# One ring of ten places for the expert weights of a mixture-of-experts layer, filled in the order of use

## The chip, the core and the metric

The kernel runs on one NeuronCore of a Trainium2 chip. The metric is the device time of one execution in microseconds (us); a kernel is judged by the median of its runs. Everything is float32.

## What is computed

One layer of an encoder trunk on 256 tokens of width 1024: a token mixer (differential attention and stick-breaking attention, behind an adaLN-conditioned RMSNorm), then a mixture of experts, then a final RMSNorm. Only the mixture of experts matters here. Each token goes to 4 of 32 experts:

```python
logits = (t @ router_w + router_b); top_val, top_idx = top_k(logits, 4); gates = softmax(top_val)
for each expert e, over the tokens xe that chose it:
    g, u = split(xe @ w_gu[e] + b_gu[e])            # w_gu[e]: 1024 x 2048
    g = minimum(g, 7); u = clip(u, -7, 7)
    y = ((u + 1) * (g * sigmoid(1.702 * g))) @ w_down[e] + b_down[e]   # w_down[e]: 1024 x 1024
    out[tokens] += gate * y
```

The weights of one expert are 12 MB (8 MB of `w_gu`, 4 MB of `w_down`), of all 32 experts 384 MB (402.7 million bytes). All of them are read, whatever the tokens choose.

## The kernel before, in words

The kernel is written engine by engine, with semaphores by hand. The token mixer comes first and ends some 400 us into the span; the expert part follows on the same buffers.

**Pieces and places.** SP (SyncE) issues all weight loads, each a piece of 2 MB: four pieces of `w_gu` and two of `w_down` per expert (`load_gu`, L378; `load_down`, L384). `gu_ring` is 16 MB: two halves of four places each. `down_ring` is 4 MB: two places. Expert e has its `w_gu` pieces in half e mod 2, and its `w_down` pieces in the two places of `down_ring`, as all experts have. So ten pieces fit at a time.

**TensorE, one expert** (`expert`, L1615). It takes the `w_gu` pieces in order (L1624; a wait on `slot_in` before each, L1634), eight k-tiles of 128 rows, with `give` of the former expert between (L1612) and `take` of the next one's tokens behind (L1582). After each second k-tile it raises `gu_used` so that a place becomes free. Then come the eight k-tiles of `w_down` (L1661; a wait on `down_in` before each half, L1659), with `down_used` behind each half. A matmul of 64 token places by 512 columns in float32 is two instructions of TensorE in the trace.

**Further passes.** An expert's main pass has 64 token places (`CAP`). If more tokens chose it, `further` (L1667) runs once for each 32 more, behind a branch on a count from memory (L346): matmuls with the same `w_gu` pieces again (L1691) and `w_down` (L1704), then the main pass's `w_down` part. The code of `further` stands in each copy of `expert`; where it isn't needed, TensorE jumps over it. With these inputs one expert, number 25 counted from 0, needs one such pass.

**TensorE's loop** (L1732) holds two experts, one for each half of `gu_ring`, and runs 16 times. VectorE and ScalarE have loops of one expert.

**The order of SP's loads.** SP issues in program order, and each issue waits until TensorE is done with the piece that stood there. For the first 16 experts the order is: `w_gu` of expert e+1, then `w_down` of expert e (L481 to L485). Around expert 16 a stretch written out moves each `w_down` piece one place ahead per expert (L486 to L493). From expert 21 on the order is `w_gu` of e, `w_down` of e (L497 to L500), where the two `w_down` pieces wait for `down_used` of the expert before. The first issue for an expert also waits for `f_gu_done`, so that no further pass still reads the place (L463 to L466).

Of the kernel before, what the change touches and what calls it, by code (L numbers as in the profile page):

```python
# [31 lines left out]
P = 128  # L32
D = 1024
T = 256
KT = D // P
# [4 lines left out]
NE, TOPK = 32, 4  # L40
# [19 lines left out]
FURTHER_BLOCKS = (T - CAP) // FCAP  # L60
PAIRS = NE // 2
TOGETHER = NE // 2

# [20 lines left out]
def build(nc, x, c, w_ada, b_ada, norm1_g, w_in, lam_q1, lam_k1, lam_q2, lam_k2, subln_g, w_pa, w_pb, w_o,  # L84
          norm2_g, router_w, router_b, w_gu, b_gu, w_down, b_down, final_g, out):
    ctx = ExitStack()
    with ctx:
# [103 lines left out]
        vt_pairs = xn[0:12, 1, 0:2 * P]  # L191
        fgb = xn[:, 0, :]
        bgu_rows = gu_ring[:, 11, 0:512]
# [140 lines left out]

        USES = [7] * 4 + [8] * 4 + [0] * 8

# [40 lines left out]
        def _(sp):  # L377
            def load_gu(expert, half, j):  # L378
                first = 8 * half + 2 * j
                sp.dma_start(gu_ring[:, first:first + 2, :].rearrange("p r n -> p (r n)"),  # L380
                             w_gu[0, bass.ds(expert, 1), j * 2 * P:(j + 1) * 2 * P, :]
                             .rearrange("a (p r) n -> p (a r n)", r=2)).then_inc(slot_in[first], 16)

            def load_down(expert, a):  # L384
                sp.dma_start(down_ring[:, 2 * a:2 * a + 2, :].rearrange("p s n -> p (s n)"),
                             w_down[0, bass.ds(expert, 1), a * 4 * P:(a + 1) * 4 * P, :]
                             .rearrange("a (p r) n -> p (a r n)", r=4)).then_inc(down_in[a], 16)

# [21 lines left out]
            for n, (w, g) in enumerate(GROUPS):  # L410
                if n < 2:
                    continue
                if n == len(GROUPS) - 1:
                    sp.wait_ge(sbpv_done, SBH)
                    for half in range(2):
                        sp.dma_start(y_sb[64 * half:64 * half + NE, :], b_down[0, :, half * 512:(half + 1) * 512]
                                     ).then_inc(bdown_in, 16)
                    for a in range(2):
                        load_down(0, a)
                    load_gu(1, 1, 0)  # L420
                if n >= 4:
# [19 lines left out]
            for j in range(4):  # L441
                if j == 2:
                    sp.wait_ge(merged_ready, 4)
                    for pair in (2, 3):
                        load_gu(1, 1, pair)
# [4 lines left out]
                load_gu(0, 0, j)  # L450
            sp.wait_ge(x1_ready, 4)
            sp.wait_ge(g2b_done, 1)
            load_gu(1, 1, 1)

            def load_item_gu(item, half):

                for j in range(4):
                    load_gu_pair(item, half, j)

            def load_gu_pair(item, half, j):  # L460

                if j == 0:
                    passes_made = sp.value_load(passes[0:1, 2, bass.ds(item - 1, 1)], min_val=1, max_val=T * TOPK // FCAP + 1)  # L463
                sp.wait_ge(gu_used, item * 8 + (2 * j - 14))
                if j == 0:
                    sp.wait_ge(f_gu_done, passes_made)  # L466
                load_gu(item, half, j)

            def load_down_half(item, a):

                sp.wait_ge(down_used, item * 2 + (a - 1))
                load_down(item, a)

            def load_item_down(item):
                for a in range(2):
                    load_down_half(item, a)

            sp.wait_ge(passes_ready, 1)
            load_item_gu(2, 0)
            load_item_down(1)  # L480
            with sp.Fori(1, TOGETHER // 2) as n:  # L481
                load_item_gu(n * 2 + 1, 1)
                load_item_down(n * 2)
                load_item_gu(n * 2 + 2, 0)
                load_item_down(n * 2 + 1)  # L485
            for step in range(4):  # L486
                item = TOGETHER + step
                for j in range(4):
                    if j == 3 - step:
                        load_down_half(item, 0)  # L490
                    load_gu_pair(item + 1, (item + 1) % 2, j)
                    if j == min(3, 4 - step - (step > 0)):
                        load_down_half(item, 1)  # L493
            load_item_down(TOGETHER + 4)
            load_item_gu(TOGETHER + 5, 1)
            load_item_down(TOGETHER + 5)
            with sp.Fori(TOGETHER // 2 + 3, PAIRS) as n:  # L497
                for half in range(2):
                    load_item_gu(n * 2 + half, half)
                    load_item_down(n * 2 + half)  # L500
            sp.wait_ge(taken_done, NE + 1)
            sp.dma_start(fgb, final_g.partition_broadcast(P)).then_inc(fg_in, 16)
# [711 lines left out]
        def _(pe):  # L1214
# [399 lines left out]

            def expert(item, half, fills):  # L1615

                count = further_count(pe, item)
                pe.wait_ge(xTe_ready, item + 1)

                def gate_up(kt, parts):  # L1620

                    for f in parts:
                        a = f % 2
                        last = M(bank[f // 2][64 * a:64 * a + 64, :], xT[:, kt % 4, kt // 4, :],  # L1624
                                 gu_ring[:, 8 * half + kt, f * 512:(f + 1) * 512],
                                 start=kt == 0, stop=kt == KT - 1, skip_group_check=True)
                    if f == 3:
                        last.then_inc(gu_used, 1)
                    elif kt == KT - 1:
                        last.then_inc(g_done, 1)  # L1630

                for kt in range(KT):
                    if kt % 2 == 0:
                        pe.wait_ge(slot_in[8 * half + kt], fills * 16 + 16 * USES[8 * half + kt])  # L1634
# [16 lines left out]
                way_back(item)  # L1651
                further_passes(pe, item, count, lambda b, k: further(item, half, fills, k))
                for kt in range(KT):
                    if kt == KT // 2:
                        take_transposed(item + 1)
                    if kt % (KT // 2) == 0:
                        pe.wait_ge(act_ready, item * 2 + (1 + 2 * kt // KT))
                    if kt % 4 == 0:
                        pe.wait_ge(down_in[kt // 4], item * 16 + 16)  # L1659
                    for a in range(2):  # L1660
                        last = M(bank[7][64 * a:64 * a + 64, :], act_sb[:, kt % 4, kt // 4, :],  # L1661
                                 down_ring[:, kt // 2, (kt % 2) * D + a * 512:(kt % 2) * D + (a + 1) * 512],
                                 start=kt == 0, stop=kt == KT - 1, skip_group_check=True)
                    if kt % 4 == 3:
                        last.then_inc(down_used, 1)

            def further(expert, half, fills, k):  # L1667

# [20 lines left out]
                for kt in range(KT):  # L1689
                    for f in range(4):  # L1690
                        last = M(bank[0][FCAP * f:FCAP * (f + 1), :], f_xT[:, kt % 2, kt // 2, :],  # L1691
                                 gu_ring[:, 8 * half + kt, f * 512:(f + 1) * 512],
                                 start=kt == 0, stop=kt == KT - 1, skip_group_check=True)
                last.then_inc(f_gu_done, 1)
# [4 lines left out]
                for kt in range(KT):  # L1699
                    if kt % 4 == 0:  # L1700
                        pe.wait_ge(down_in[kt // 4], expert * 16 + 16)
                    for a in range(2):
                        row = 64 * a + FCAP * (kt % 2)
                        last = M(bank[7][row:row + FCAP, :], f_act_sb[:, kt % 4, kt // 4, :],  # L1704
                                 down_ring[:, kt // 2, (kt % 2) * D + a * 512:(kt % 2) * D + (a + 1) * 512],
                                 start=kt < 2, stop=kt >= KT - 2, skip_group_check=True)
                last.then_inc(f_down_done, 1)
# [23 lines left out]
            pe.wait_ge(passes_ready, 1)  # L1731
            with pe.Fori(0, PAIRS) as n:  # L1732
                for half in range(2):
                    expert(n * 2 + half, half, n + 1)
            give(NE - 1)
# [19 lines left out]
```

## Time and profile before

| | |
|---|---|
| median of 3 runs | 1336.17 us (1335.73 to 1341.78) |
| span of the profiled execution | 1337.1 us |
| TensorE matmul (PE) busy | 1281.4 us, 96% |
| VectorE (DVE) busy | 518.3 us, 39% |
| ScalarE (ACT) busy | 187.3 us, 14% |
| read from HBM | 476.1 MB, 357 GB/s over the span |

The time of the profiled execution is not given apart from its span; the span, from the first to the last instruction, stands 0.9 us above the median of the runs. The expert part begins at 407 us (first matmul with `w_gu` of expert 0) and ends with the last instruction, so it is 930 us of the span. PE is the matmul part of TensorE, PEld its weight load; SPq is SP's sequencer issuing DMAs. A busy PE may still be a PE that is paced by its loads: whether it stands still shows in the idle time before an instruction, and in the chain of waits.

### The profile page before, as it was taken

To read this page: it belongs to the slowest core of one execution; us is meant where nothing else is said; L and a number is where in the kernel's file an instruction comes from. 1 tells how busy PE (TensorE), PEld (TensorE's weight loads), DVE (VectorE), ACT (ScalarE), POOL (GpSimd) and SP (SyncE) were. 2 spreads that over 40 slices of the span, in tenths; PEclk is the share of its full clock that TensorE was granted. 3 is DMA by queue.
4 is the path that set the end of the run, shared out by engine and by line. 5 is a ranking of instruction groups with operands and counts; after the bars stand their busy time and mean duration, and the time that the engine had idled before them with its cause. 6 is when DMAs were issued, how large, how long until landed. Compare 5 with 4: busy or idle time off the path is not lost.

```text
span 1337.1 us, 16781 instructions
## 1 busy us (share of the span) xinstructions
PE 1281.4 (96%) x5991; PEld 592.9 (44%) x5992; DVE 518.3 (39%) x1160; ACT 187.3 (14%) x381; POOL 15.6 (1%) x48
## 2 busy tenths in 40 slices
PE   6999999999999999999999999999999999899997
PEld 4866866778753333333333333333333333233332
DVE  3132665332234443444334334433434334334344
ACT  2101322332021001100001000000100011001002
POOL 0000000110000000000000000000000000000000
PEclk9999999999999999999999999999999999999999
DMA  9858675316678999999999999999999999799994
GB/s 355 318 189 291 223 245 186 126 64 230 231 287 318 425 428 428 428 428 429 428 428 429 429 428 429 428 428 428 414 429 428 428 429 428 315 430 427 428 430 210
DMA packets 59183, 477.55 MB, mean 357 GB/s; under 512 B 4991, under 2 KB 5076, under 8 KB 32532
## 3 DMA queue, kind: packets, MB, share of 16 engines
q1 hardware_dynamic: 58852, 476.11, 86.7%
q10 hardware_dynamic: 304, 1.06, 0.2%
q8 instruction: 19, 0.31, 0.1%
q14 instruction: 8, 0.07, 0.0%
HBM read 476.10 MB, written 1.05 MB: 357 GB/s over the span
## 4 chain that ended last, share of the span: by engine, by line
PE 74%; DMA 20%; DVE 3%; issue 1%; ACT 1%; SPq 0%; ACTq 0%; DVEq 0%
PE bank L1624 23%; DMA down_ring<-in_w_down 17%; PE bank L1661 15%; PE bank L1306 11%; PE bank L1452 4%; PE bank L1299 4%; PE bank L1612 3%; PE bank L1590 3%; DMA gu_ring<-in_w_gu 3%; PE bank L1354 2%; PE bank L1515 2%; PE bank L1582 1%; PE bank L1413 1%; DMA xres<-in_x 1%; DVE scratch L1137 1%
## 5 line engine op out<-in xcount | busy, mean ns | idle before, releaser
L1624 PE MATMUL bank<-gu_ring,scratch 128*64 128x512 f32 x2048 | 461.2, 597 | 1.7 <-DVE scratch L1067 1.6
L1624 PEld LDWEIGHTS bank<-gu_ring,scratch 128*64 128x64 f32 x2048 | 143.7, 137 | 286.3 <-issue 285.3
L1661 PE MATMUL bank<-down_ring,scratch 128*64 128x512 f32 x1024 | 235.5, 602 | 23.2 <-DMA down_ring<-in_w_down 18.0
L1306 PE MATMUL bank<-gu_ring 128*128 128x256 f32 x640 | 143.8, 381 | 0.0
L1661 PEld LDWEIGHTS bank<-down_ring,scratch 128*64 128x64 f32 x1024 | 71.0, 137 | 145.5 <-issue 133.5
L1306 PEld LDWEIGHTS bank<-gu_ring 128*128 128x128 f32 x640 | 119.8, 190 | 18.6 <-issue 1.3
L718 ACT ACTIVATE scratch<-bank 128x512 f32<-128x512 f32 x32 | 19.1, 597 | 686.5 <-PE bank L1624 686.5
L1125 DVE TENSOR_TENSOR scratch<-bank,bgu 128x512 f32<-128x512 f32 x32 | 22.1, 692 | 219.7 <-PE bank L1590 219.7
L1093 DVE TENSOR_TENSOR xres<-xres,bank 128x512 f32<-128x512 f32 x132 | 81.9, 682 | 60.1 <-PE bank L1612 60.1
L1590 PEld LDWEIGHTS bank<-ident,scratch 128*128 128x128 f32 x392 | 41.1, 140 | 79.5 <-issue 26.0
L1582 PE MATMUL bank<-xn,onehot 128*64 128x512 f32 x264 | 69.6, 605 | 0.0
L1066 DVE TENSOR_TENSOR scratch<-bank,a 128x512 f32<-128x512 f32 x33 | 22.8, 692 | 114.5 <-PE bank L1590 114.5
L1612 PE MATMUL bank<-scratch,back 64*128 64x512 f32 x264 | 65.6, 615 | 0.8 <-DVE scratch L1143 0.8
L1590 PE MATMUL bank<-ident,scratch 128*128 128x128 f32 x392 | 64.2, 286 | 0.7 <-ACT scratch L734 0.7
L1452 PE MATMUL bank<-gu_ring 128*128 128x256 f32 x256 | 56.4, 380 | 0.0
L1299 PE MATMUL bank<-gu_ring 128*128 128x512 f32 x128 | 55.8, 592 | 0.0
L1143 DVE TENSOR_TENSOR scratch<-bank,scratch 128x512 f32<-128x512 f32 x32 | 22.1, 692 | 79.8 <-PE bank L1661 79.8
L1452 PEld LDWEIGHTS bank<-gu_ring 128*128 128x128 f32 x256 | 48.3, 190 | 7.2 <-ACT gu_ring L671 0.5
L1113 DVE TENSOR_SCALAR gated<-iota,r,gates 128x64 f32<-128x64 f32 x128 | 40.3, 315 | 8.5 <-DVE gated L1113 6.1
L1612 PEld LDWEIGHTS bank<-scratch,back 64*128 64x128 f32 x264 | 22.7, 186 | 43.2 <-issue 41.5
L1135 DVE TENSOR_TENSOR scratch<-bank,bgu 128x256 f32<-128x256 f32 x64 | 26.9, 421 | 24.7 <-PE bank L1590 24.7
L1299 PEld LDWEIGHTS bank<-gu_ring 128*128 128x128 f32 x128 | 24.0, 190 | 28.2 <-issue 28.2
(265 smaller groups left out, 824.8 us busy)
## 6 DMA issues: line engine op xcount, KB each, us to landing
gu_ring<-in_w_gu SPq DMA_DIRECT2D x128, 2048.0 KB, 23.9
down_ring<-in_w_down SPq DMA_DIRECT2D x64, 2048.0 KB, 17.2
gu_ring<-in_w_in SPq DMA_DIRECT2D x32, 1024.0 KB, 7.8
gu_ring<-in_w_ada SPq DMA_DIRECT2D x16, 1024.0 KB, 7.0
down_ring<-in_w_ada SPq DMA_DIRECT2D x8, 512.0 KB, 10.6
gu_ring<-in_w_ada SPq DMA_DIRECT2D x8, 512.0 KB, 11.6
gu_ring<-in_w_pa SPq DMA_DIRECT2D x4, 1024.0 KB, 6.4
gu_ring<-in_w_pb SPq DMA_DIRECT2D x4, 1024.0 KB, 6.4
```

What stands on the lines that cost most here:

```text
L1093: V.tensor_tensor(xres[:, tt, cols], xres[:, tt, cols], bank[4 + n][:, :], ALU.add).then_inc(given_added, 1)
L1113: last = V.tensor_scalar(gated[:, tt, a, :], iota[:], r1[:, tt, bass.ds(item, 1)], gates[:, tt, bass.ds(item, 1)], ALU.is_equal, ALU.mult)
L1135: own.then(V.tensor_tensor(u, blocks(3)[:, :, a, :], u_bias, ALU.add))
L1299: last = M(dst[:, :], hT[:, kt, h * P:(h + 1) * P], group_chunk(group, kt // 4)[:, kt % 4, :], start=kt == 0, stop=kt == KT - 1)
L1306: last = M(dst[:, b * T:(b + 1) * T], group_chunk(group, kt // 4)[:, kt % 4, cols], hT[:, kt, :], start=kt == 0, stop=kt == KT - 1)
L1354: last = M(dst[:, b * T:(b + 1) * T], group_chunk(POS["in", g], a)[:, kt % 4, (2 * h + b) * P:(2 * h + b + 1) * P], hT[:, kt, :], start=kt ...
L1452: last = M(dst[:, b * T:(b + 1) * T], group_chunk(group, kt // 4)[:, kt % 4, (2 * h + b) * P:(2 * h + b + 1) * P], src[:, kt, :], start=kt ...
L1582: last = M(bank[4][64 * a:64 * a + 64, :], onehot[:, tt, :], xn[:, tt, a * 512:(a + 1) * 512], start=tt == 0, stop=tt == TT - 1, skip_grou ...
L1590: last = nc.tensor.transpose(bank[b][:, j * P:(j + 1) * P], src[:, j * P:(j + 1) * P], ident[:])
L1612: M(bank[4 + n][:, :], back[rows_, tt * P:(tt + 1) * P], y_sb[rows_, :], start=True, stop=True).then_inc(given_done, 1)
L1624: last = M(bank[f // 2][64 * a:64 * a + 64, :], xT[:, kt % 4, kt // 4, :], gu_ring[:, 8 * half + kt, f * 512:(f + 1) * 512], start=kt == 0 ...
L1661: last = M(bank[7][64 * a:64 * a + 64, :], act_sb[:, kt % 4, kt // 4, :], down_ring[:, kt // 2, (kt % 2) * D + a * 512:(kt % 2) * D + (a + ...
```

## The change

The two halves of `gu_ring` and the two places of `down_ring` become one ring of ten places. Piece n of the whole run is piece n mod 6 of expert n div 6 (four of `w_gu`, then two of `w_down`), and it goes to place `PLACES[n mod 10]`. Since 30 pieces are the least common multiple of 6 and 10, the places repeat every five experts: TensorE's loop holds five copies of `expert` and runs 6 times, and two more copies stand behind it. SP's loads are one function, `refill`: it waits until piece n-10 has been used, and issues piece n; there is no other order. The first ten pieces go to the same places at the same points of the program as before. The waits on landings (`wait_piece`) count the uses of each place. `final_g` is loaded to a free place of the ring, behind `down_used` of expert 30, instead of to `xn`. ScalarE's, VectorE's and GpSimd's programs are the same but for where `final_g` is read.

```diff
-PAIRS = NE // 2
-TOGETHER = NE // 2
+PIECES, GU_PIECES = 6, 4
+PLACES = (0, 1, 2, 3, 8, 9, 4, 5, 6, 7)
+CYCLE = 5
...
-        fgb = xn[:, 0, :]
+        fgb = gu_ring[:, 4, 0:D]
...
+        def area(place):
+
+            return gu_ring[:, 2 * place:2 * place + 2, :] if place < 8 else down_ring[:, 2 * place - 16:2 * place - 14, :]
...
+        def wait_piece(eng, piece, rounds):
+
+            place = place_of(piece)
+            eng.wait_ge(place_in(place), rounds * 48 + 16 * (USES[place] + piece // len(PLACES) + 1))
...
+            def refill(piece, rounds):
+
+                before_it = piece - len(PLACES)
+                former, i = before_it // PIECES + rounds * CYCLE, before_it % PIECES
+                if i == 0:
+                    passes_made = sp.value_load(passes[0:1, 2, bass.ds(former + 1, 1)], min_val=1, max_val=T * TOPK // FCAP + 1)
+                if i < GU_PIECES:
+                    sp.wait_ge(gu_used, former * 8 + (2 * i + 2))
+                else:
+                    sp.wait_ge(down_used, former * 2 + (i - GU_PIECES + 1))
+                if i == 0:
                     sp.wait_ge(f_gu_done, passes_made)
-                load_gu(item, half, j)
...
+                load_piece(rounds * CYCLE + piece // PIECES, piece % PIECES, place_of(piece))
 
             sp.wait_ge(passes_ready, 1)
...
+            for piece in range(len(PLACES), CYCLE * PIECES):
+                refill(piece, 0)
+            with sp.Fori(1, NE // CYCLE) as n:
+                for piece in range(CYCLE * PIECES):
+                    refill(piece, n)
+            for piece in range(NE % CYCLE * PIECES):
+                refill(piece, NE // CYCLE)
+            sp.wait_ge(down_used, 2 * NE - 2)
             sp.dma_start(fgb, final_g.partition_broadcast(P)).then_inc(fg_in, 16)
...
-            with pe.Fori(0, PAIRS) as n:
-                for half in range(2):
-                    expert(n * 2 + half, half, n + 1)
+            with pe.Fori(0, NE // CYCLE) as n:
+                for e in range(CYCLE):
+                    expert(e, n)
+            for e in range(NE % CYCLE):
+                expert(e, NE // CYCLE)
             give(NE - 1)
```

**SP, the loads that take the first places TensorE frees** (expert 0's four `w_gu` places, then its two `w_down` places; in brackets the semaphores waited for). Before:

```order
L463 TENSOR_LOAD passes [waits passes_ready]
L463 ISA x2
L380 DMA gu_ring<-in_w_gu 128x4096 [waits f_gu_done,gu_used]
L380 DMA gu_ring<-in_w_gu 128x4096 [waits gu_used] x3
L385 DMA down_ring<-in_w_down 128x4096 [waits down_used] x2
```

Now:

```order
L477 TENSOR_LOAD passes [waits passes_ready]
L477 ISA x2
L401 DMA gu_ring<-in_w_down 128x4096 [waits f_gu_done,gu_used]
L401 DMA gu_ring<-in_w_down 128x4096 [waits gu_used]
L401 DMA gu_ring<-in_w_gu 128x4096 [waits gu_used] x2
L401 DMA down_ring<-in_w_gu 128x4096 [waits down_used] x2
```

The events waited for are the same six in the same order. What is loaded at them differs: the `w_down` pieces of expert 1 come ahead of the `w_gu` pieces of expert 2.

**TensorE, the end of the second copy of `expert`** (its `w_down` part, with the transposes of the next expert's tokens between). Before, the loop ends there:

```order
L1661 MATMUL bank<-down_ring,scratch 64x512 x8
L1590 MATMUL bank<-ident,scratch 128x128 x4
L1661 MATMUL bank<-down_ring,scratch 64x512 x8
L1732 REGISTER_ALU
L1732 COMPARE_AND_BRANCH
L1612 MATMUL bank<-scratch,back 128x512 x4
```

Now the third of five copies follows, and the `w_down` pieces lie in `gu_ring`:

```order
L1668 MATMUL bank<-gu_ring,scratch 64x512 x8
L1583 MATMUL bank<-ident,scratch 128x128 x4
L1668 MATMUL bank<-gu_ring,scratch 64x512 x8
L360 ISA
L360 TENSOR_LOAD passes
L360 ISA x2
L351 REGISTER_ALU
L1632 MATMUL bank<-gu_ring,scratch 64x512 x8
L1605 MATMUL bank<-scratch,back 128x512 x4
```

The matmuls of one expert are as many and as large as before; the branch back comes after five experts instead of two.

## Rows read from the trace of the kernel before

**Rows 1.** The page, section 2: GB/s in 40 equal slices of the span.
```profile
GB/s 355 318 189 291 223 245 186 126 64 230 231 287 318 425 428 428 428 428 429 428 428 429 429 428 429 428 428 428 414 429 428 428 429 428 315 430 427 428 430 210
```

**Rows 2.** Busy time by stretch: length, each engine's us (x instructions), PEclk, DMA share, GB/s.
```profile
430.00:930.00 500.00, 480.34 (x2218) 165.99 (x2216) 195.54 (x459) 44.92 (x85) 0.00 (x0) 1.00 1.01 428
930.00:950.00 20.00, 19.81 (x97) 6.74 (x93) 7.06 (x16) 2.65 (x5) 0.00 (x0) 1.00 0.97 401
950.00:1130.00 180.00, 178.77 (x829) 60.14 (x826) 72.29 (x170) 17.64 (x33) 0.00 (x0) 1.00 1.01 429
1150.00:1160.00 10.00, 8.24 (x42) 3.02 (x40) 4.62 (x8) 0.00 (x0) 0.00 (x0) 1.00 0.28 80
1160.00:1316.00 156.00, 155.06 (x721) 52.17 (x717) 62.75 (x148) 14.99 (x28) 0.00 (x0) 1.00 1.00 427
```

**Rows 3.** The same view: one early expert, one later expert, the first 400 us.
```profile
428.64:456.02 27.38, 27.19 (x127) 9.21 (x127) 11.15 (x27) 2.65 (x7) 0.00 (x0) 1.00 1.01 424
...
538.14:565.51 27.37, 27.18 (x126) 9.20 (x127) 11.09 (x27) 2.64 (x7) 0.00 (x0) 1.00 1.01 429
...
0.00:400.00 400.00, 384.92 (x1791) 285.00 (x1792) 145.22 (x275) 93.90 (x201) 15.61 (x48) 1.00 0.63 228
```

**Rows 4.** The chain that ended last: start us, us, what.
```profile
620.26 3.65 PE bank L1661 x16
...
628.26 24.61 DMA down_ring<-in_w_down
...
912.82 3.65 PE bank L1661 x16
...
1088.15 35.68 DMA gu_ring<-in_w_gu
1123.87 2.80 PE bank L1624 x12
```

**Rows 5.** L380's issue at 1088.1 and L385's last issue: duration ns, start; time to landing.
```profile
L380 SPq DMA_DIRECT2D gu_ring<-in_w_gu x1: 333/333/333, 1088.1 to 1088.1; - x1
...
DMA to landing us min/median/max: 35.7/35.7/35.7
...
L385 SPq DMA_DIRECT2D down_ring<-in_w_down x1: 332/332/332, 1298.8 to 1298.8; - x1
...
DMA to landing us min/median/max: 19.2/19.2/19.2
```

**Rows 6.** PE's timeline: start us, us, line, operation, count, idle before and its releaser.
```profile
1117.54 9.13 PE L1624 MATMUL bank<-gu_ring,scratch 128*64 128x512 f32 x40
...
1135.52 7.07 PE L1691 MATMUL bank<-gu_ring,scratch 128*32 128x512 f32 x64 [1.14 <-DVE scratch L1167]
...
1322.38 3.65 PE L1661 MATMUL bank<-down_ring,scratch 128*64 128x512 f32 x16
```

**Rows 7.** SP's timeline around the further pass: issues of weight loads.
```profile
1108.26 4.51 SPq L385 DMA_DIRECT2D down_ring<-in_w_down  x2
1114.04 2.08 SPq L380 DMA_DIRECT2D gu_ring<-in_w_gu  x4
1157.79 4.51 SPq L385 DMA_DIRECT2D down_ring<-in_w_down  x2
```

**Rows 8.** Busy time over the stretch of the further pass.
```profile
1131.95:1153.96 22.01, 15.23 (x128) 5.39 (x129) 7.45 (x20) 2.28 (x6) 0.00 (x0) 1.00 0.88 373
```

**Rows 9.** DMA queues of 0:400, 400:520, 514:518, then 520:1337: packets, MB, share of 16 engines.
```profile
q8 instruction: 14, 0.23, 0.2%
...
q8 instruction: 5, 0.08, 0.3%
...
q8 instruction: 1, 0.02, 1.6%
...
q1 hardware_dynamic: 23585, 338.68, 97.6%
q14 instruction: 1, 0.01, 0.0%
```

**Rows 10.** Landing time of L385's issues at 487.22 and at 514.59.
```profile
DMA to landing us min/median/max: 13.9/13.9/13.9
...
DMA to landing us min/median/max: 15.9/15.9/15.9
```

More of the change, by code:

```diff
@@ L377, in _, with load_piece, load_first @@
         def _(sp):
[L378 to L387, printed above, removed]
+            def load_piece(expert, i, place):
+                if i < GU_PIECES:
+                    src = w_gu[0, bass.ds(expert, 1), i * 2 * P:(i + 1) * 2 * P, :].rearrange("a (p r) n -> p (a r n)", r=2)
+                else:
+                    src = w_down[0, bass.ds(expert, 1), (i - GU_PIECES) * 4 * P:(i - GU_PIECES + 1) * 4 * P, :].rearrange(
+                        "a (p r) n -> p (a r n)", r=4)
+                sp.dma_start(area(place).rearrange("p r n -> p (r n)"), src).then_inc(place_in(place), 16)
+            def load_first(piece):
+                load_piece(piece // PIECES, piece % PIECES, place_of(piece))
             def load_group_chunk(n, h):
@@ L417, in _ @@
                                      ).then_inc(bdown_in, 16)
-                    for a in range(2):
-                        load_down(0, a)
-                    load_gu(1, 1, 0)
+                    for piece in (4, 5, 6):
+                        load_first(piece)
                 if n >= 4:
@@ L443, in _ @@
                     sp.wait_ge(merged_ready, 4)
-                    for pair in (2, 3):
-                        load_gu(1, 1, pair)
+                    for piece in (8, 9):
+                        load_first(piece)
                 if j < 3:
@@ L449, in _ @@
                     sp.wait_ge(mixed_done, 4)
-                load_gu(0, 0, j)
+                load_first(j)
             sp.wait_ge(x1_ready, 4)
             sp.wait_ge(g2b_done, 1)
[L453 to L465, printed above, removed]
-                    sp.wait_ge(f_gu_done, passes_made)
-                load_gu(item, half, j)
@@ L1613, in give, with expert, rows_of, gu_columns @@
                       ).then_inc(given_done, 1)
-            def expert(item, half, fills):
+            def expert(e, rounds):
+                item = rounds * CYCLE + e
                 count = further_count(pe, item)
+                def rows_of(i):
+                    return area(place_of(e * PIECES + i))
+                def gu_columns(kt, f):
+                    return rows_of(kt // 2)[:, kt % 2, f * 512:(f + 1) * 512]
+                def wait_down(a):
+                    wait_piece(pe, e * PIECES + GU_PIECES + a, rounds)
+                def down_columns(kt, a):
+                    first = (kt % 2) * D + a * 512
+                    return rows_of(GU_PIECES + kt // 4)[:, kt % 4 // 2, first:first + 512]
                 pe.wait_ge(xTe_ready, item + 1)
@@ L1651, in expert @@
                 way_back(item)
-                further_passes(pe, item, count, lambda b, k: further(item, half, fills, k))
+                further_passes(pe, item, count, lambda b, k: further(item, gu_columns, down_columns, wait_down, k))
                 for kt in range(KT):
```

58 lines of the change are left out of this document (16 added, 42 removed).

## The prediction, made before the changed kernel was run

> **What bounds the kernel now.** I read the bandwidth by slice first. From the fourteenth slice on, the DMA engines move some 428 GB/s nearly without a break, for the whole expert part [rows 1]. TensorE is busy 96% of the span too, so two resources look full, and the question is which one sets the end. The table by stretch sharpens it: 428 GB/s from 430 to 930 us, and only two dents afterwards, 401 GB/s in 930 to 950 and 80 GB/s in 1150 to 1160 [rows 2]. At 428 GB/s one expert's 12.58 million bytes take 29.4 us. TensorE alone needs 27.37 us for an expert, early and later [rows 3]. So loads are the slower side by 2.0 us per expert, and TensorE runs freely only while it lives on pieces that landed before it wanted them.
>
> The chain of waits shows how that store is used up. Until 628 us it is all TensorE; then it goes nine times through a load of `w_down`, the first 24.61 us long; after that TensorE alone again, until it goes once through a load of `w_gu` at 1088.15, and from 1123.87 on TensorE to the end [rows 4]. From expert 7's `w_down` part (620.26) to expert 17's (912.82) are 292.6 us, where ten free experts take 273.7: the nine waits cost 18.9 us in all. That is what the change seems to aim at. But one row decides what it is worth: the load at 1088.15 is the fourth `w_gu` piece of expert 25; it lands at 1088.1 + 35.7 = 1123.8 [rows 5]. TensorE's group of 40 matmul instructions for that expert begins at 1117.54 and wants this piece after 28 of the 40, so 1117.5 + 6.2 = 1123.7 (9.13 less the wait is 8.80, by 28/40) [rows 6]. TensorE and the piece arrive together, **after** TensorE has lost its 18.9 us. Without that loss it would stand there at 1104.8 and wait 19 us for the same piece. It is piece 154 of the run in either order (25 whole experts and four), and nothing in the change makes the DMA engines faster.
>
> **Part by part.** *The order of the loads.* SP waits for the same events of TensorE, a place set free by each; so the engines are fed at least as early. What a load brings is now always what is wanted next. The waits at experts 8 to 16 go, 18.9 us of TensorE's time. They return before expert 25, since the supply line hasn't moved. What moves it: the dent at 930 to 950, where the written-out stretch of SP's order had the queue run empty, was 20 x (1 - 401/428) = 1.3 us. With it gone piece 154 lands at 1122.5. Gain 1.3 us.
>
> *The further pass.* In it TensorE frees nothing for 22.0 us [rows 8]. SP sent the four pieces of expert 26 at 1114.04, then stood on `w_down` until 1157.79, though expert 25's `w_gu` places were free from the end of L1691 at 1142.6 [rows 6, 7]. The ring refills them from 1142.6 on. The dent at 1150 to 1160, 10 x (1 - 80/428) = 8.1 us of supply, goes. But who waits for it? Nobody: from 1123.87 to the end the chain has no load in it. The last piece lands at 1298.8 + 19.2 = 1318.0 and is wanted at 1322.4 [rows 5, 6]. With the dent gone it has 12 us of room instead of 4. Gain 0. After expert 25 TensorE's own path of 1337.1 - 1123.8 = 213.3 us sets the end, and it is unchanged.
>
> *`final_g`.* Loaded behind `down_used` of expert 30, at the back of the queue, used some 10 us after the last matmul. Cost 0, hidden by the last expert's `w_down` part; without that cover it would be one load of half a megabyte.
>
> *Register work.* TensorE's waits have a register added in some places, one or two instructions per expert. The matmuls stand back to back in the trace though such instructions lie between them already, so 0; above, 0.1 us per expert for the six experts that count, 0.6.
>
> Up to here the sum is -1.3: 1336.2 - 1.3 = **1334.9 us**.
>
> *TensorE's code.* The first 400 us are 1791 + 1792 instructions in a straight line, and the instruction queue q8 brought 14 packets of 0.23 MB together [rows 3, 9]: 3583/14 = 256 instructions to a packet of 16 KB. A copy of `expert` has 254 instructions in its main pass [rows 3], 257 in `further` [rows 8] and some 30 for registers and branches, in all 2.14 packets. The loop of two copies is 4.3 packets. q8 brings five packets between 400 and 520 and none at all afterwards, in fourteen rounds of the loop [rows 9]: a body of 4.3 packets is kept. The loop of five copies is 10.7 packets. Whether that is kept no row shows. I take it that it isn't, since it is over twice the size that the trace shows to be kept; then each of the six rounds loads its 11 packets anew.
>
> The Trainium skill, "Runtime: NRT & Kernel Launch", section "Instruction fetch mechanics", speaks against the change here: it gives TensorE's instruction memory as 128 KiB, 2048 instructions, a FIFO refilled in blocks of 16 KiB. By that the two-expert body (some 1,100) stays and the five-expert body (some 2,740) does not. The block size and the kept loop agree with the trace. The same section says that memory has only two lines and a taken branch out of them stops the engine for a fetch; the trace has no packet in fourteen rounds of 4.3, so for TensorE the measurement decides against it.
>
> What does a reload cost? TensorE itself: at its first pass through the code, with the DMA engines full, expert 0 to 1 took 27.38 us, a later one 27.37 [rows 3]; so 0 for loading ahead. The supply line: a packet takes 1.6% of 16 engines over 4 us = 1.0 us of one DMA engine [rows 9]. A weight piece is spread over 16 engines and lands with the slowest, and behind 428 GB/s no engine has room to catch up. In the kernel before one packet more or less was harmless: around the packet of 515 us, landings follow each other as ever, (514.6 + 15.9) - (487.2 + 13.9) = 29.4 us [rows 10]; so it fell on an engine that wasn't the latest. With eleven packets in each round that stops being so. If the same packets fall on the same engines each round, an engine is set back 1.0 us a round: six loads by the time of piece 154, +6.0 us. If they spread evenly, five rounds and the start of the sixth are 58 packets, x 1.0/16 = 3.6; at a weight packet's price (16,384 bytes at 428/16 GB/s = 0.61 us), 2.2. Above, 1.5 us each where a packet also holds up those behind it, 9. I take 6.0, the same code coming by the same way each round. Piece 154 then lands at 1128.5, and TensorE's 213.3 us follow.
>
> Sum: 1336.2 - 1.3 + 6.0 = **1341 us**, 0.35% slower.
>
> **The rivals.** *Kept, or loaded at no cost.* The body stays, or its packets fall on engines with room. For it: one packet at 515 us cost nothing. Against: 10.7 against 4.3. Time: 1334.9.
>
> *TensorE stops for its code.* This is the case on the other side of "no change". Each branch over `further` skips more than one packet's length, and the branch back goes to code that was dropped. In experts 26 to 31 TensorE alone sets the end, so each stop there counts in full, while before expert 25 the 2.0 us of load wait per expert cover them. Those six experts are 12.8 packets; at 1.0 us for each that isn't there in time, 1341 + 13 = 1354; if only the six branches wait, 1347. It decides from the point where a packet comes later than TensorE's sequencer reaches it. Against: expert 0's first pass, with the same jump over unread code, lost 0.01 us.
>
> *All of the 18.9 us.* If supply weren't the bound at expert 25, the nine waits' time would be kept: 1336.2 - 18.9 = 1317. Needed is a landing of piece 154 19 us earlier; rows 2 leave 1.3 us of unused supply before it.
>
> **How the numbers follow.** About 0.5% (6.7 us) is what a measurement of this kernel can tell from no change: the bounds are 1329.5 and 1342.9. Forecast (code reloaded, paid by supply; 1337 to 1345): 0.55, of which 0.23 above 1342.9, for the dearer packet. Kept or free: 0.22, same. TensorE stops: 0.20, slower. The 18.9 us kept: 0.03, faster. So faster 0.03, same 0.22 + 0.32 = 0.54, slower 0.43. The range reaches from just under the free case, 1334, to 1350, which takes in a part of the third case; the rest and the fast case are left out.
>
> **What would show it.** Right: no load wait before expert 14; from then on one of about 2 us at each expert on a `w_gu` piece, not `w_down`; the fourth piece of expert 25 landing between 1126 and 1132; SP's issues going on at the end of L1691; no dent at 1150; TensorE ending some 208 to 214 us after that landing; q8 with 60 to 75 packets, eleven in each round. The free case would show that piece at 1122 to 1123. TensorE stopping for code would show as idle or "issue" time at the first matmuls behind the branches in experts 26 to 31, and more than 27.4 us for each. Wrong altogether if the chain goes through `w_down` loads again, or q8 shows 19 packets and the time is still above 1338.

## The result, and the profile after

The changed kernel takes 1427.49 us (median of 4 runs, 1424.03 to 1433.29), the kernel before, run beside it, 1337.67 us (1335.73 to 1341.78): ratio 1.067, 95% interval 1.0645 to 1.070. It is slower by 90 us, where the forecast was 1341 us with a range of 1334 to 1350. (The kernel before was run again beside each batch below, with medians of 1337.0 to 1338.8; ratios are taken within a batch.)

The page of the changed kernel, sections 1, 2 and 3:

```profile
span 1427.7 us, 16771 instructions
PE 1321.7 (93%) x5991; PEld 600.0 (42%) x5992; DVE 518.1 (36%) x1160; ACT 187.3 (13%) x381; POOL 15.6 (1%) x48
...
GB/s 355 275 204 293 229 265 129 80 98 348 186 305 420 427 427 365 373 429 425 426 370 429 427 423 323 417 426 425 382 369 427 429 426 152 340 429 426 427 278 31
...
q8 instruction: 94, 1.54, 0.4%
```

Against [rows 1] the bandwidth now has dents at regular distances, and one slice at 152: the DMA engines are no longer full, they wait for places. TensorE is busy for 1321.7 us instead of 1281.4 with the same 5991 matmul instructions, 40.3 us more. And q8 has 94 packets where it had 19 [rows 9].

The chain that ended last (start us, us, what), the pieces without an instruction, with the next matmul group at three of them. No load is in it after 500 us; before, it went through ten: nine of `w_down` and one of `w_gu` [rows 4].

```profile
515.32 2.85 issue
518.16 5.34 PE bank L1668 x14
...
548.23 3.30 issue
551.52 6.24 PE bank L1668 x16
...
561.93 4.42 issue
566.36 5.35 PE bank L1632 x16
...
1315.25 3.23 issue
...
1348.25 3.31 issue
```

There are 17 such pieces in the chain, three in each of the first five rounds and two in the last. In a round they stand at the same three places: two matmul instructions into the `w_down` part of the fourth copy, at the start of that part in the fifth copy (it follows the branch over `further` in both), and at the branch back to the first copy. TensorE's waits show them as idle time with no releaser (us in total, times, longest):

```profile
PE bank L1668 <- issue: 45.0, 13, 4.6
...
PE bank L1632 <- issue: 21.2, 5, 5.0
...
PE bank L1583 <- issue: 3.0, 6, 1.0
```

One of the thirteen in the first row, 0.9 us behind the further pass, stands in the kernel before too; the seventeen long stops are 65.3 us together. The last row is a short stop of 0.2 to 1.0 us in the third copy of each round, inside its `w_down` part.

TensorE's timeline at the fourth copy, then at the fifth and around the branch back after the first round:

```profile
514.25 1.07 PE L1668 MATMUL bank<-gu_ring,scratch 128*64 128x512 f32 x2 [0.19 <-DVE scratch L1130]
518.16 5.34 PE L1668 MATMUL bank<-gu_ring,scratch 128*64 128x512 f32 x14 [2.85 <-issue]
...
546.60 0.44 PE L1594 MATMUL bank<-ident,gated 128*128 128x128 f32 x2
551.52 6.24 PE L1668 MATMUL bank<-gu_ring,scratch 128*64 128x512 f32 x16 [4.48 <-issue]
557.69 0.66 PE L1583 MATMUL bank<-ident,scratch 128*128 128x128 f32 x4
558.28 3.65 PE L1668 MATMUL bank<-gu_ring,scratch 128*64 128x512 f32 x16
```

The same 16 matmuls take 6.24 us behind a stop of 4.48 us and 3.65 a little later. Behind the next branch back the granted clock is 0.64 (last row of the next view), where it is 1.00 in a free expert [rows 3]: the clock had gone to its lower level, 1.2 GHz, after TensorE had stood idle, for a part of the stretch. Busy time by stretch, in the columns of [rows 2]: the second and third round of five experts, then 3.5 us shortly behind the second branch back.

```profile
566.36:719.91 153.55, 141.18 (x631) 47.05 (x631) 55.38 (x130) 13.21 (x25) 0.00 (x0) 0.97 0.99 409
719.91:877.35 157.44, 144.73 (x631) 47.98 (x631) 55.40 (x130) 13.21 (x25) 0.00 (x0) 0.95 0.98 405
...
721.50:725.00 3.50, 3.50 (x12) 0.90 (x8) 0.00 (x0) 0.00 (x0) 0.00 (x0) 0.64 0.87 365
```

Five free experts would take 136.9 us; a round takes 153 to 157. The 90.6 us between the two spans begin with 2.7: the first matmul of the expert part starts at 409.85 for 407.17, ahead of all that was changed. The other 87.9 lie in experts 0 to 24 and in experts 25 to the end, before and after in the same columns:

```profile
407.17:1112.07 704.90, 683.73 (x3150) 234.70 (x3152) 276.96 (x652) 66.08 (x125) 0.00 (x0) 1.00 1.00 423
1112.07:1337.10 225.03, 207.93 (x1020) 70.25 (x1016) 90.89 (x211) 24.61 (x51) 0.00 (x0) 0.99 0.90 379
...
409.85:1187.09 777.24, 713.86 (x3150) 237.36 (x3151) 279.13 (x659) 66.05 (x125) 0.00 (x0) 0.96 0.97 404
1187.09:1427.70 240.61, 215.20 (x1018) 72.35 (x1018) 88.55 (x204) 24.59 (x51) 0.00 (x0) 0.96 0.71 295
```

Experts 0 to 24 take 72.3 us more, the rest 15.6. Matmuls are slower by 30.1 + 7.3 = 37.4 us; the stops are 65.3 + 3.0 = 68.3 us of idle time that was not there before; and TensorE's 18.0 us of waits for `w_down` loads are gone. 37.4 + 68.3 - 18.0 = 87.7. Nothing large is left to explain. (2.9 of the 40.3 us of TensorE's busy time lie ahead of the expert part.)

### The profile page after: what moved, and what is told of

It reads as the page before. It is cut to its first block, busy times and chain, and to the rows that moved or that the text cites. A ratio compares the mean times of both kernels' runs of the same rounds, so it can differ in the third digit from the quotient of the medians.

```text
span 1427.7 us, 16771 instructions
## 1 busy us (share of the span) xinstructions
PE 1321.7 (93%) x5991; PEld 600.0 (42%) x5992; DVE 518.1 (36%) x1160; ACT 187.3 (13%) x381; POOL 15.6 (1%) x48
## 4 chain that ended last, share of the span: by engine, by line
PE 89%; issue 5%; DVE 4%; DMA 1%; ACT 1%; DVEq 0%; ACTq 0%
PE bank L1632 32%; PE bank L1668 18%; PE bank L1299 10%; PE bank L1605 4%; PE bank L1583 4%; PE bank L1445 4%; PE bank L1292 4%; PE bank L1347 2%; PE bank L1575 2%; PE bank L1508 2%; DVE scratch L1128 1%; DVE scratch L1130 1%; DVE scratch L1129 1%; PE bank L1406 1%; DMA xres<-in_x 1%
## 5 line engine op out<-in xcount | busy, mean ns | idle before, releaser
L1632 PE MATMUL bank<-gu_ring,scratch 128*64 128x512 f32 x1664 | 384.4, 609 | 22.8 <-issue 21.2
L1668 PE MATMUL bank<-gu_ring,scratch 128*64 128x512 f32 x800 | 210.3, 656 | 46.6 <-issue 44.1
L1632 PEld LDWEIGHTS bank<-gu_ring,scratch 128*64 128x64 f32 x1664 | 117.0, 139 | 263.3 <-issue 263.3
L1668 PEld LDWEIGHTS bank<-gu_ring,scratch 128*64 128x64 f32 x800 | 60.3, 149 | 162.4 <-issue 157.9
L1299 PEld LDWEIGHTS bank<-gu_ring 128*128 128x128 f32 x640 | 119.8, 190 | 18.6 <-issue 1.3
L1632 PE MATMUL bank<-down_ring,scratch 128*64 128x512 f32 x384 | 87.1, 595 | 0.0
L1668 PE MATMUL bank<-down_ring,scratch 128*64 128x512 f32 x224 | 51.2, 598 | 2.9 <-DVE scratch L1130 2.0
L1445 PEld LDWEIGHTS bank<-gu_ring 128*128 128x128 f32 x256 | 48.3, 190 | 7.2 <-ACT gu_ring L664 0.5
L1632 PEld LDWEIGHTS bank<-down_ring,scratch 128*64 128x64 f32 x384 | 26.5, 137 | 53.5 <-issue 53.5
L1106 DVE TENSOR_SCALAR gated<-iota,r,gates 128x64 f32<-128x64 f32 x128 | 40.2, 314 | 8.5 <-DVE gated L1106 6.1
```

The lines of the kernel that those rows point to most:

```text
L1106: last = V.tensor_scalar(gated[:, tt, a, :], iota[:], r1[:, tt, bass.ds(item, 1)], gates[:, tt, bass.ds(item, 1)], ALU.is_equal, ALU.mult)
L1299: last = M(dst[:, b * T:(b + 1) * T], group_chunk(group, kt // 4)[:, kt % 4, cols], hT[:, kt, :], start=kt == 0, stop=kt == KT - 1)
L1445: last = M(dst[:, b * T:(b + 1) * T], group_chunk(group, kt // 4)[:, kt % 4, (2 * h + b) * P:(2 * h + b + 1) * P], src[:, kt, :], start=kt ...
```

## The experiments

Two theories stood after the result. **Theory L**: a body longer than TensorE keeps is loaded anew in each round, and TensorE stops where a branch reaches code that isn't there. **Theory W**: the ring holds TensorE, by its waits or its places. Theory J is a form of L in which a branch over code stops TensorE, kept or not.

### The pass's code once in the loop

```diff
-                further_passes(pe, item, count, lambda b, k: further(item, gu_columns, down_columns, wait_down, k))
+                if e == 0:
+                    further_passes(pe, item, count, lambda b, k: further(item, gu_columns, down_columns, wait_down, k))
```

> The changed kernel, with the code of the further pass standing only in the first of the five copies of expert (expert 25 is that copy; the other six copies have no branch and no such code). All that is computed for these inputs is the same. The loop body falls from 10.7 to 6.3 packets of code. Theory L (TensorE keeps about 8 packets of 16 KB; a longer body is loaded anew each round, and it stops where a jump outruns the load): no stops, q8 some 25 packets, time 1334 to 1338 us, that is the value of the ring alone, -1.3 us. Theory W (the ring itself, its waits or its places, holds TensorE): time stays near 1427. Theory J (the stops come from jumping over code, kept or not): six of seven jumps are gone, the rest of the reloading stays, time about 1350.

Measured: 1353.36 us, 1.010 of the kernel before (1.007 to 1.013); q8 has 69 packets. Its chain has these pieces without an instruction, one at each branch back:

```profile
546.10 3.87 issue
...
688.55 4.00 issue
...
1118.91 3.43 issue
```

74 us of the 90 went with code that is never run in those copies, the ring untouched: theory W is out. The time is the one that theory J named, about 1350, but the place of what is left isn't: five stops at the branch back. The stops at the fourth and fifth copy are gone with their branches, though reloading went on, so loading alone, in a line, stops next to nothing here (0.5 us once, at 1309). But a body of 6.3 packets isn't kept (sizes of loop bodies are counted from the program's instructions, 256 to a packet): my figure of 8 was too high.

### The kernel before with longer loops

Four copies in the loop:

```diff
-            with pe.Fori(0, PAIRS) as n:
-                for half in range(2):
-                    expert(n * 2 + half, half, n + 1)
+            with pe.Fori(0, PAIRS // 2) as n:
+                for copy in range(4):
+                    expert(n * 4 + copy, copy % 2, n * 2 + (copy // 2 + 1))
```

> The kernel before, its rings and loads untouched, with four copies of expert in TensorE's loop, run 8 times, instead of two, run 16 times. Body 8.6 packets. Theory L with 8 packets kept: reloaded each round, q8 80 to 90 packets, stops at the fourth copy's jump and at the branch back, 8 to 12 us in each of 8 rounds less the 18.9 us of load waits that they take the place of: 1380 to 1420 us. Theory W: no change, 1337. If more than 8.6 packets are kept: stops in the first round only, 1337.

Measured: 1409.77 us, 1.053 (1.047 to 1.059), q8 100 packets. The old rings and the old order of loads, and most of the loss is there (71 us of the 90). The fourth copy's branch and the branch back, in TensorE's timeline:

```profile
508.89 0.64 PE L1661 MATMUL bank<-down_ring,scratch 128*64 128x512 f32 x1 [0.19 <-DVE scratch L1137]
512.64 6.60 PE L1661 MATMUL bank<-down_ring,scratch 128*64 128x512 f32 x15 [3.12 <-issue]
...
526.49 4.53 PE L1624 MATMUL bank<-gu_ring,scratch 128*64 128x512 f32 x10 [3.08 <-issue]
```

Then two copies, and matmuls behind a branch that is always taken over them:

```diff
+                never = further_count(pe, n)
+                with pe.If(never > FURTHER_BLOCKS - 1):
+                    for _ in range(180):
+                        M(bank[7][:, :], xT[:, 0, :, :].rearrange("p a s -> p (a s)"), gu_ring[:, 0, 0:512], start=True, stop=True)
```

> The kernel before, with 180 matmuls that are never run behind a branch at the end of the loop of two copies; body 7.1 packets. Theory L with 8 packets kept: loaded once, one stop in the first round, 1337 to 1340 us, q8 some 22 packets. If what is kept is under 7.1 packets: a reload in each of 16 rounds, 1380 or more.

> The same with 280 matmuls that are never run; body 8.7 packets. Nothing else differs from the run with 7.1. Theory L with 8 packets kept: the branch over them and the branch back each reach code that is gone, two stops of 3 to 5 us with a slow clock behind in each of 16 rounds, 6 to 10 us a round, so 96 to 160 less the 18.9 us of load waits: 1410 to 1480 us. If a stop comes from the branch itself and not from the length: the same time as with 7.1 packets.

> The kernel before with 64 matmuls that are never run at the end of the loop of two copies; body 5.3 packets, in 6 blocks. Theory L: between the 4.3 that are kept and the 6.3 that aren't. Kept: q8 about 20 packets, 1337 us. Not kept: 90 packets or more and 1400 to 1440 us.

> The same with 110 matmuls that are never run; body 6.0 packets, in 7 blocks. Theory L with the limit between 4.3 and 6.3: kept: q8 about 21, 1337 us; not kept: 90 packets, 1400 to 1440 us. Since a body of 6.3 in 7 blocks was loaded anew in each round, I expect not kept.

| matmuls never run | body, packets | q8 packets | median us | ratio to before, interval |
|---|---|---|---|---|
| 0 | 4.3 | 19 | | |
| 64 | 5.3 | 20 | 1341.97 | 1.002 (1.000 to 1.004) |
| 110 | 6.0 | 20 | 1342.65 | 1.003 (1.0015 to 1.0045) |
| 180 | 7.1 | 95 | 1442.78 | 1.078 (1.072 to 1.083) |
| 280 | 8.7 | 95 | 1444.73 | 1.079 (1.073 to 1.085) |

The length of the body decides, and sharply: with 6.0 packets the code is kept, with 7.1 it isn't, in kernels that differ in nothing else. The body of 6.3 that wasn't kept is another one, five copies with the pass's code once; it puts the limit below 6.3 only if the count alone matters. From 7.1 to 8.7 more length costs nothing more. I had expected 7.1 to be kept and 6.0 not: both wrong, in opposite directions. The body with 6.0 packets stops TensorE once, in the first round (the chain's row is `464.57 4.67 issue`), and never again before the further pass, though it takes the same branches 15 times more; that one stop is enough for the 4 us that the kernel loses. So theory J is out too: a branch over kept code is free. With 7.1 packets the stop at the loop's end is 11.9 us long and comes in every other round:

```profile
519.12 3.65 PE L1661 MATMUL bank<-down_ring,scratch 128*64 128x512 f32 x16
534.71 5.27 PE L1624 MATMUL bank<-gu_ring,scratch 128*64 128x512 f32 x16 [11.93 <-issue]
```

Not all of such a body is read again each time: between 586 and 642 us, a whole round, q8 moves no packet, and two rounds bring nine.

### The ring alone

With a limit of 6 packets the ring can be had without reloading: the code of the pass stands only in expert 25's copy, behind the loop.

```diff
-            with pe.Fori(0, NE // CYCLE) as n:
+            with pe.Fori(0, 5) as n:
                 for e in range(CYCLE):
                     expert(e, n)
-            for e in range(NE % CYCLE):
-                expert(e, NE // CYCLE)
+            for item in range(25, NE):
+                expert(item % CYCLE, item // CYCLE)
```

> The changed kernel's ring and loads, with TensorE's code arranged otherwise: the loop of five copies has no code of the further pass and runs 5 times (experts 0 to 24); experts 25 to 31 stand behind it in a straight line, and only expert 25's copy has the code of the pass. The same is computed for these inputs. The loop body is 5.2 packets, in 6 blocks. Theory L, as mended by the last runs (a body of 4.3 packets is kept, one of 6.3 isn't): if 5.2 is kept, no stops, q8 28 to 30 packets, load waits of 2 us at experts 16 to 25, and 1334 to 1336 us, the ring alone. If 5.2 is not kept: one stop of about 4 us and 1.7 us of slow clock at each of 4 branches back, of which the load waits before expert 25 cover 19 us, so 1336 to 1340.

Measured: 1336.84 us, 0.9994 of the kernel before (0.9978 to 1.0009), q8 28 packets, no stop before expert 25. The span is 1335.1 us. The chain, and TensorE's timeline at expert 25:

```profile
845.49 41.84 DMA down_ring<-in_w_gu
...
1021.02 42.50 DMA gu_ring<-in_w_gu
...
1079.83 42.42 DMA gu_ring<-in_w_gu
1122.29 2.80 PE bank L1632 x12
```

```profile
1114.22 6.23 PE L1632 MATMUL bank<-gu_ring,scratch 128*64 128x512 f32 x28
1122.29 2.80 PE L1632 MATMUL bank<-gu_ring,scratch 128*64 128x512 f32 x12 [1.85 <-DMA gu_ring<-in_w_gu]
```

This is the first half of the prediction, row for row. TensorE's load waits, ten of up to 1.8 us, stand on `w_gu` pieces and start at expert 16, and the fourth piece of expert 25 lands at 1079.83 + 42.42 = 1122.25 (forecast 1122.5). The dent at 1150 is filled:

```profile
1150.00:1160.00 10.00, 9.06 (x46) 3.25 (x44) 3.92 (x7) 0.00 (x0) 0.00 (x0) 1.00 1.00 423
```

It had 80 GB/s in [rows 2], and it brought nothing to the end, as forecast. The ring alone is worth 1 to 2 us, which these runs can't tell from none.

### Code in a straight line

The same without a loop on TensorE, `for item in range(NE): expert(item % CYCLE, item // CYCLE)`, 48 packets of code, the pass's code in expert 25 alone:

> The same ring with no loop on TensorE at all: 32 copies of expert in a straight line, the code of the further pass in expert 25's alone; 48 packets of code, read once. No branch is taken before expert 25. Theory L (code read ahead in a straight line costs TensorE nothing, only jumps stop it): no stops, about 47 packets in q8. The supply line carries 27 packets of code before expert 25's fourth piece; at 1.0 us of one engine each, spread over engines, it comes 1 to 3 us late: 1336 to 1338 us. If loading code stops TensorE even in a straight line: above 1345.

Measured: 1346.01 us, 1.006 (1.004 to 1.0085), above my 1338 and, by the number alone, in the case "loading code stops TensorE". The trace says otherwise: TensorE stops nowhere for code before expert 25. But the supply line does pay: the fourth piece of expert 25 is issued at 1081.9 and lands 43.7 us later, at 1125.6, for 1122.25, some 3.3 us later, with 20 packets of code more ahead of it. By my estimate that is 3.3/20 x 16 = 2.6 us of one engine for a packet if they spread evenly, not 1.0. The spans are 1341.7 and 1335.1, and the other half of these 6.6 us is the clock (the medians stand 9.2 apart, and no profile shows the rest):

```profile
1125.63 4.49 PE L1632 MATMUL bank<-gu_ring,scratch 128*64 128x512 f32 x12 [2.10 <-DMA gu_ring<-in_w_gu]
...
1149.89 5.22 PE L1710 MATMUL bank<-down_ring,scratch 128*32 128x512 f32 x32 [2.47 <-issue]
```

The first group took 2.80 us behind a wait of 1.85 above and takes 4.49 behind one of 2.10. The second took 3.64 there, behind the same 2.47 us.

Then all copies with the code of the pass and the branch over it, still without a loop, 82 packets:

> The ring with 32 copies of expert in a straight line, each with the code of the further pass and the branch over it, and no branch back: 82 packets of code, read once. It tells what makes the forward branches stop TensorE. From one copy to the next the branch moves by 0.11 of a block. In the changed kernel the branches of the first two copies of a round cost nothing, those of the fourth and fifth 2.7 to 4.6 us, the seventh nothing. Place theory (a branch stops where it stands in certain places of a block): stops at some 2 to 4 of each 9 experts, 8 to 12 in all, each 3 to 5 us with the slow clock behind, so 1345 to 1375 us. Wear theory (each jump over unread code eats into what is read ahead, and only the branch back restores it): every branch from the fourth copy on stops, 28 x 4.5 us less 19 us of load waits: 1430 to 1450 us.

Measured: 1355.9 us, 1.013 (1.0095 to 1.017). Stops of 3.2 to 4.4 us stand at the branches of experts 4, 5, 15, 16 and 26, five where I had said 8 to 12; shorter losses, 0.5 to 1.5 us, stand beside them (3, 6, 14, 17, 27, 28), and next to none at 0 to 2, 7 to 13 and 18 to 24. TensorE's timeline behind the branches of experts 3, 4 and 5, and the instruction queue from 539 to 541 us:

```profile
509.73 3.65 PE L1668 MATMUL bank<-gu_ring,scratch 128*64 128x512 f32 x16
514.07 0.66 PE L1583 MATMUL bank<-ident,scratch 128*128 128x128 f32 x4 [0.68 <-issue]
...
537.78 1.08 PE L1668 MATMUL bank<-gu_ring,scratch 128*64 128x512 f32 x4
542.08 4.31 PE L1668 MATMUL bank<-gu_ring,scratch 128*64 128x512 f32 x12 [3.22 <-issue]
...
569.61 0.44 PE L1594 MATMUL bank<-ident,gated 128*128 128x128 f32 x2
574.11 5.24 PE L1668 MATMUL bank<-down_ring,scratch 128*64 128x512 f32 x16 [4.06 <-issue]
...
q8 instruction: 1, 0.02, 3.3%
```

So whether a branch over unread code stops TensorE depends on where in its 16 KB block it stands, the place theory; the wear theory would have had 28 stops. The rows say more than I had asked of them. TensorE goes on 4.1 to 4.3 us behind the branch each time, whatever it had left to do: 3.65 us of matmuls and a stop of 0.68, 1.08 and 3.22, none and 4.06. Each time q8 moves one packet in between, here from 539 to 541, 1 to 3 us before TensorE goes on. The plain reading is that the next block is only fetched once the branch has jumped past code, and that the stop is what is left of some 4 us when the code at hand has run out; where a block's end falls isn't in the trace, so this is a reading and no proof. It accounts for the distance too: from expert 3 to 4 the stop moves by twelve matmul instructions and their weight loads, 24 instructions or 0.09 of a block (I had counted 0.11), and after 256/24, some eleven experts, the stops come again.

### Another order of the experts

If the end is set by the last piece that TensorE waits for, the place of the further pass in the order matters: TensorE's 22 us in it are time in which the DMA engines get ahead. The experts are taken as 10 to 31, then 0 to 9, so that expert 25 comes sixteenth; weights are loaded in that order, and router columns and biases are placed so:

```diff
+TURN = 10
+TURNED = ((slice(0, NE - TURN), slice(TURN, NE)), (slice(NE - TURN, NE), slice(0, TURN)))
...
-w_gu[0, bass.ds(expert, 1), i * 2 * P:(i + 1) * 2 * P, :]
+w_gu[0, bass.ds((expert + TURN) % NE, 1), i * 2 * P:(i + 1) * 2 * P, :]
```

> The kernel of the run with the pass outside the loop, with the experts taken in the order 10 to 31, then 0 to 9 (weights, router columns and biases loaded so), so that expert 25 and its further pass come sixteenth instead of twenty-sixth. TensorE's loop of five copies runs 3 times, then 17 copies stand in a straight line, 38 packets of code in all; SP's loads are written out without a loop. The same is computed. Supply theory (the end is set by the last piece that TensorE has to wait for, plus TensorE's work behind it): in the sixteenth place TensorE is still living on its store, the pass costs 22 us of TensorE's time while the engines go on, and the next waits come only near the last expert. The fourth w_gu piece of the last expert lands at about 1299, 27 us are behind it: 1325 to 1328 us, plus 1 to 3 for code in the supply line: 1325 to 1331, faster by 6 to 11. If place of the pass doesn't matter: 1335 to 1339.

> The kernel before with the same order of experts and SP's loads written out without loops (their order as before); TensorE's code as before, 18.9 packets. Supply theory: the load order of the first half binds from expert 8 on by 2 us each, so some 16 us of the store are lost before the pass, where the engines may run dry; the last piece still bounds the end: 1326 to 1336 us, not faster than the ring so turned. If the ring has no worth of its own, the two turned kernels are the same within 2 us.

Measured: the ring so turned 1331.62 us, 0.9958 of the kernel before (0.9945 to 0.9972); the kernel before so turned 1344.28 us, 1.0048 (1.0035 to 1.0061). The turned ring beats both kernels, by 5.4 us over the one before; the turned kernel before came out 8 us above my range. It runs free past expert 25; its last load wait is the fourth `w_gu` piece of its last expert, at 1302.4, 3 us behind my 1299, with 38 packets of code:

```profile
1259.74 42.64 DMA gu_ring<-in_w_gu
1302.42 2.79 PE bank L1638 x12
```

The turned kernel before has four slices of lower bandwidth in the middle, which I had left out:

```profile
GB/s 355 315 202 299 212 240 175 125 64 255 235 286 337 429 429 429 429 428 428 428 429 428 429 430 428 315 376 382 390 430 430 429 429 429 427 428 429 429 429 235
```

Those are (4 x 428 - 315 - 376 - 382 - 390)/428 x 33.6 us = 19.5 us of supply lost where SP stands on `w_down` during the pass and in the written-out stretch. There the ring is worth 12.7 us, since there the supply that it saves is still wanted at the end: the turned kernel before waits for a `w_gu` piece that lands at 1275.3 + 40.2 = 1315.5, 13.1 us after the turned ring's last. (The two also differ in TensorE's code, but neither stops for code in its loop.) This version is made for inputs where expert 25 alone needs a pass, as are all above that drop the pass's code from some copies.

## Why the prediction was wrong

*What bounds the kernel.* Right, and shown: with the reload taken away the ring gives 1336.84 us for the 1334.9 forecast, with the landing of piece 154 at 1122.25 for 1122.5, load waits of up to 1.8 us at each expert from 16 on, no dent at 1150. That the nine waits' 18.9 us would come back as waits for `w_gu` was right too.

*The five copies are loaded anew.* Right: 94 packets in q8, 13 in the second round (I had said eleven a round and 60 to 75 in all). The count of a copy was a little off: 254 + 257 + 30 instructions are 2.11 packets and not 2.14, which changes nothing here.

*"TensorE itself: ... so 0 for loading ahead."* This is the step that failed. I took one row, expert 0 to 1 at 27.38 us on the first pass through the code, as proof that a branch over unread code costs nothing. The row was true of the first two copies, and it stays true of them in every later round. But a branch stops TensorE or doesn't according to its place in a block; the fourth and fifth copies stand where it does, which two copies could not show. And no row of the kernel before had a branch back to code that was gone. Measured: 65.3 us idle at 17 stops of 2.7 to 5.0 us, and 3.0 us at six short ones, where I had 0.

*The rival "TensorE stops for its code"* named the mechanism and both places, at 0.20, and was itself too cheap, 1347 to 1354. It counted stops only in experts 26 to 31, since "before expert 25 the 2.0 us of load wait per expert cover them". TensorE's load waits are 18.0 us in all, and experts 0 to 24 alone brought 72.3 + 18.0 = 90.3. Cover is a sum that is used up; I compared per expert and not in total. It also had 1.0 us per packet, what the packet itself takes of an engine, where TensorE stood for 3 to 5 us.

*The clock.* Not in any of my cases: 37.4 us, more than a third of what came in, are slower matmuls, at a granted clock of 0.96 over the expert part for 1.00. That nearly all of it lies behind the stops is read from groups such as the two above, not summed. It was to be read before: in the kernel before, the same sixteen matmuls took 5.35 us behind a wait for a load and 3.65 elsewhere:

```profile
887.91 5.35 PE L1661 MATMUL bank<-down_ring,scratch 128*64 128x512 f32 x16 [1.92 <-DMA down_ring<-in_w_down]
```

*The supply line's price*, +6.0 us, could not show in the changed kernel, where TensorE was later than any load. In the straight-line kernel a cost of this kind did: 3.3 us for 20 packets. At that rate the 58 packets of the prediction would have cost some 10 us, an estimate, so the term was rather too small; whether packets fall on one engine or on all, no run tells.

The Trainium skill, "Runtime: NRT & Kernel Launch", section "Instruction fetch mechanics", says that a taken branch whose target isn't in the window of fetched code forces a fetch before execution goes on. The stops at the branch back and in the fifth copy agree; in the fourth, two matmul instructions behind the branch still ran before the stop. I had set that rule aside on the evidence of two copies. Its 2048 instructions, 8 blocks, are more than a loop body may have here: 6.0 blocks were kept, 6.3 and 7.1 were not.

What stays open: why the limit lies between 6.0 and 6.3 packets (7.1, if only the padded kernels count) and not at 8 (blocks read ahead beyond the loop's end would do it, but no run tells), and why a body of 7.1 stops for 11.9 us only every other round and reads nothing in between.

## What to carry to other kernels

Unrolling a loop to make indices static has a price in code: count the instructions of the body, with those behind branches that are hardly ever taken, against what the engine is seen to keep, here 6 packets of 256 instructions for TensorE (more were not kept in any run), and look at the instruction queue's packet count before and after. The stops cost about one and a half times their length here, 68.3 + 37.4 us for 68.3, because the clock falls behind them. And before pricing a saved wait, find the piece that is waited for last and ask whether it comes any earlier; slack elsewhere is a total, not an allowance per step.

## What the runs showed of the hardware that I had not expected

TensorE keeps a loop body of 6.0 packets of 16 KB (some 1,540 instructions by count) and reads one of 6.3 and one of 7.1 again; the step from 6.0 to 7.1 costs 100 us on a loop of two experts, and a body of 8.7 no more than one of 7.1. Code read in a straight line did not stop TensorE in the kernel without a loop, not even behind 428 GB/s of weights, but 20 packets of it made a weight piece land 3.3 us later. A branch over a packet's length of unread code stopped it for 3.2 to 4.4 us at some places, shortly or not at all at others: in three branches in a row TensorE went on 4.1 to 4.3 us behind the branch, whatever it could do in between.
